# The down projection of a gated MLP, with products as the outer loop and output tiles inside

## The reference, cut to what matters

```python
def conv_ffn(h, w_up_l, conv_w_l, conv_b_l, w_down_l, buf):
    u = h @ w_up_l
    up = jnp.concatenate([buf.astype(u.dtype), u], axis=1)
    c = conv_b_l
    for j in range(CONV_W):
        c = c + up[:, j:j + L] * conv_w_l[j]
    a, b = jnp.split(c, 2, axis=-1)
    y = (jax.nn.silu(a) * b) @ w_down_l
    return y, up[:, -(CONV_W - 1):]
# per layer: x += RMSNorm_post(conv_ffn(RMSNorm_pre(x), ...)); everything in float32
```

## Time and profile before

| | before |
|---|---|
| median of 3 runs | 3350.73 us |
| the profiled execution, device time | 3351.13 us |
| its span in the trace | 3349.3 us |
| TensorE matmul busy | 3053.3 us, 91% |
| VectorE busy | 2233.6 us, 67% |
| ScalarE busy | 1498.5 us, 45% |
| GpSimd busy | 1177.3 us, 35% |
| DMA | 309.67 MB, mean 92 GB/s |

### The profile page before, as it was taken

One profiled execution on the slowest core, in us unless ns is written; L12 is line 12 of the kernel. 1 busy time (PEld: TensorE's weight loads), 2 busy tenths in 40 slices (PEclk: granted clock), 3 DMA queues, 4 the chain that ended last, 5 costly groups with the idle time before them and its releaser, 6 DMA issues. The chain is left out here.

```text
span 3349.3 us, 57862 instructions
## 1 busy us (share of the span) xinstructions
PE 3053.3 (91%) x23292; PEld 2903.8 (87%) x23292; DVE 2233.6 (67%) x3027; ACT 1498.5 (45%) x2616; POOL 1177.3 (35%) x664
## 2 busy tenths in 40 slices
PE   8999999999699999768889999999986999997677
PEld 8999789987599999768789997899876999997676
DVE  7887755443687777665587877563446877776665
ACT  6442554343455555433345426553434555554322
POOL 1111330111555555544411113301135555545443
PEclk9999999999799999889999999999998999998888
DMA  5112342216222223222321122421162222231223
GB/s 183 46 52 61 95 170 77 69 51 226 98 77 77 78 86 100 73 84 83 109 85 46 54 77 84 165 83 57 51 233 91 87 85 77 77 127 45 82 77 123
DMA packets 123304, 309.67 MB, mean 92 GB/s; under 512 B 9888, under 2 KB 69536, under 8 KB 119456
## 3 DMA queue, kind: packets, MB, share of 16 engines
q1 hardware_dynamic: 122752, 305.91, 27.4%
q10 hardware_dynamic: 288, 0.06, 0.0%
HBM read 245.91 MB, written 54.75 MB: 90 GB/s over the span
## 5 line engine op out<-in xcount | busy, mean ns | idle before, releaser
L325 PE MATMUL ps<-hh,w_hi 128*128 128x258 f32 (+3 forms) x4320 | 1352.0, 313 | 199.7 <-issue 73.2
L326 PE MATMUL ps<-hl,w_hi 128*128 128x258 f32 (+3 forms) x4320 | 1322.0, 306 | 0.0
L327 PE MATMUL ps<-hh,w_lo 128*128 128x258 f32 (+3 forms) x4320 | 1320.8, 306 | 0.0
L325 PEld LDWEIGHTS ps<-hh,w_hi 128*128 128x128 f32 x4320 | 835.3, 193 | 227.0 <-issue 167.7
L326 PEld LDWEIGHTS ps<-hl,w_hi 128*128 128x128 f32 x4320 | 837.4, 194 | 3.1 <-issue 0.5
L327 PEld LDWEIGHTS ps<-hh,w_lo 128*128 128x128 f32 x4320 | 834.7, 193 | 0.0
L310 POOL TENSOR_TENSOR w_lo<-w_raw,w_hi 128x1024 fp32r<-128x1024 f32 x134 | 349.8, 2614 | 1365.0 <-ACT w_hi L302 1365.0
L2262 POOL TENSOR_TENSOR w_lo<-w_lo_f,w_hi 128x512 fp32r<-128x512 f32 (+1 forms) x272 | 380.1, 1410 | 403.6 <-DVE w_lo_f L2921 301.9
L2262 POOL TENSOR_TENSOR w_lo<-w_raw,w_hi 128x512 fp32r<-128x512 f32 (+1 forms) x204 | 319.4, 1567 | 339.3 <-ACT w_hi L2625 336.2
L2625 ACT ACTIVATE w_hi<-w_lo_f 128x512 fp32r<-128x512 f32 (+1 forms) x272 | 167.8, 617 | 431.0 <-DVE w_lo_f L2921 430.8
L325 PE MATMUL ps<-Y_r,w_hi 128*128 128x258 f32 x1056 | 301.1, 285 | 16.4 <-ACT xT L2648 14.1
(11 more groups left out here) (381 smaller groups left out, 5085.4 us busy)
## 6 DMA issues: line engine op xcount, KB each, us to landing
w_raw<-in_w_stream SPq DMA_DIRECT2D x284, 512.0 KB, 3.6
gates<-f_c SPq DMA_DIRECT2D x44, 516.0 KB, 2.8
hl_f<-gates SPq DMA_DIRECT2D x24, 516.0 KB, 5.6
out_y_cols<-xT SPq DMA_DIRECT2D x6, 1376.0 KB, 8.4
xT<-out_y_cols SPq DMA_DIRECT2D x2, 4128.0 KB, 13.6
Y<-out_y_cols SPq DMA_DIRECT2D x12, 688.0 KB, 6.5
mem_keys<-in_cache_mem_k SPq DMA_DIRECT2D x6, 1024.0 KB, 5.3
Y<-in_cache_mem_k SPq DMA_DIRECT2D x6, 1024.0 KB, 8.0
```

The lines of the kernel that those rows point to most:

```text
L325: nc.tensor.matmul(out, whi, mhi, start=start, stop=False, skip_group_check=reopened)
L326: nc.tensor.matmul(out, whi, mlo, start=False, stop=False, skip_group_check=reopened)
L327: return nc.tensor.matmul(out, wlo, mhi, start=False, stop=stop, skip_group_check=reopened)
```

## The change

1. In the down part the order becomes group, product, output pair. A slot is one product of one group (`D_ORDER`: P_T1, P_22, P_11, P_T2, P_T3, P_T4, P_21); inside it the four output pairs `f` run for A and B, each pair and half in a PSUM bank of its own (bank 2f+p). A column operand is used in one slot only; when its slot is over, its gates for the next group are loaded, and combined and split in the slots that follow, by lists (`TODO`, `HIGHS`). All low parts of the column side in the down part are VectorE's.
2. The weight sums of the down part are made by GpSimd in units 2 to 21 of the up part, from raw weights loaded to the free part of `xT`, and kept in DRAM (`sums`). The down part loads each of its blocks by itself (`load_down`), the sums from there.
3. P_T2 lands in a buffer of its own (`Q`) and is merged into three quarters of the output by VectorE in the last group (`merge`).
4. The last slot runs all A steps before the B steps; the squares are taken by quarters in the last two slots, and the sums over partitions of the A quarters are put between the B steps.
5. In the up part's last unit (n = 21) VectorE combines the first operand of the down part (`combine_gates(0, P_T1, ..)`) right behind the gate, and the conv pieces are one behind the other.

```diff
+        sums = nc.dram_tensor("sums", (F_PAIRS * N_GROUPS, 4, P, 4 * P), F32, kind="Internal").ap()
...
+                    def load_down(d):
+                        g, c, f = DOWN[d]
+                        u, w = F_PAIRS * g + f, P * depth_in(g)
+                        sp.wait_ge(f_wlo, N_UP + d - 3 if d >= 4 else N_UP - 1 + d // 2)
...
+                            sp.wait_ge(f_kept, 16 * (u + 1))
+                            src = sums[u, (P_T1, P_T2, P_22, P_T3).index(c)][:, 0:w]
+                        sp.dma_start(down_raw(d), src).then_inc(f_draw[d % 4], 16)
...
+                    def load_gates(g, q):
...
+                            if q == "spare":
+                                if g:
+                                    sp.wait_ge(f_t, down_t_no(g - 1, P_T2, p))
+                                else:
+                                    sp.wait_ge(f_conv, 2 * (FT - 1))
...
+                                sp.wait_ge(f_step, STEP_NO[g - 1, q, F_PAIRS - 1, p] if g else STEP_NO[FT - 1, q, p])
...
+                    for n in range(FT):
+                        if n < FT - 1:
                             load_raw(n + 1, 0)
                             load_raw(n + 1, 1)
+                        else:
+                            for d in range(4):
+                                load_down(d)
+                        if n:
                             store_gate(n - 1)
+                        if n == 1:
+                            load_staged(0)
+                        for k in halves_in(n):
+                            if k % 2:
+                                store_sums(k // 2)
+                                if k // 2 + 1 < F_PAIRS * N_GROUPS:
+                                    load_staged(k // 2 + 1)
+                    for i, q in enumerate((P_T1, "spare", P_11, P_T2, P_22, P_T3, P_21, P_T4)):
+                        load_gates(0, q)
+                        if i >= 3 and i < 7:
+                            load_down(i + 1)
+                    for at_slot in range(NP * N_GROUPS):
+                        g, at = divmod(at_slot - 1, NP)
+                        if at_slot and g < LAST_G:
+                            load_gates(g + 1, D_ORDER[at])
+                            if at == 1:
+                                load_gates(g + 1, "spare")
+                        for d in range(4 * at_slot + 8, min(4 * at_slot + 12, len(DOWN))):
+                            load_down(d)
...
+                def halves_in(n):
+                    return [k for k in range(2 * F_PAIRS * N_GROUPS) if n == 2 + k * (FT - 2) // (2 * F_PAIRS * N_GROUPS)]
...
+                    def sum_half(k):
+                        i, half = divmod(k, 2)
+                        pool.wait_ge(f_stage, 32 * (i + 1))
...
+                    for n in range(FT):
                         if n:
                             low_block(n, P_T4)
+                        for k in halves_in(n):
+                            sum_half(k)
+                        if n < FT - 1:
                             for c in range(NP - 1):
                                 low_block(n + 1, c)
+                    for d in range(len(DOWN)):
+                        low_down(d)
+                    add_squares()
...
+                    def down_step(d, p):
+                        g, c, f = DOWN[d]
+                        nk, at = depth_in(g), D_ORDER.index(c)
+                        pe.wait_ge(f_wlo, N_UP + d + 1)
+                        if f == 0:
+                            pe.wait_ge(f_lo, down_low_no(g, c, p))
+                        if at:
+                            wait_down_read(pe, g, D_ORDER[at - 1], f, p)
...
+                    for p in (A, B):
+                        for f in range(F_PAIRS):
+                            down_step(len(DOWN) - F_PAIRS + f, p)
+                            if (f, p) == (1, B):
+                                end.sum_post(pe, 1)
+                                end.sum_post(pe, 0)
...
+                        if last:
+                            high_down(0)
+                            high_down(1)
+                            high_gates(0, P_T1, A)
+                            high_gates(0, P_T1, B)
+                            high_down(2)
+                            high_down(3)
...
+                    for n in range(1, FT):
+                        last = n == FT - 1
+                        conv(n - 1, 0)
+                        conv(n - 1, 1)
+                        gate(n - 1)
+                        if last:
+                            combine_gates(0, P_T1, A)
+                            combine_gates(0, P_T1, B)
+                        else:
                             combine_block(n + 1, P_T1)
                         add_out(n, P_22, A)
                         add_out(n, P_22, B)
...
                         add_out(n, P_T3, A)
                         add_out(n, P_T3, B)
+                        if last:
+                            low_gates(0, P_T1, A)
+                            low_gates(0, P_T1, B)
...
+                    c_, l_ = combine_gates, low_gates
+                    TODO = {1: [(l_, 0, P_11), (c_, 0, P_T3), (c_, 0, P_T2)], 2: [(c_, 0, P_T4), (l_, 0, P_T2), (l_, 0, P_T3)],
...
+                    for g in range(2, N_GROUPS):
+                        TODO |= {NP * g - 5: [(c_, g, P_T1)], NP * g - 4: [(l_, g, P_T1), (l_, g, P_22)], NP * g - 3: [(l_, g, P_11)],
+                                 NP * g - 2: [(c_, g, P_T3), (c_, g, P_T2)], NP * g - 1: [(c_, g, P_T4), (l_, g, P_T2)],
+                                 NP * g: [(l_, g, P_T3), (l_, g, P_T4)], NP * g + 1: [(l_, g, P_21)]}
+                    for at_slot in range(NP * N_GROUPS):
+                        g, at = divmod(at_slot, NP)
+                        c, todo = D_ORDER[at], [(*w, p) for w in TODO.get(at_slot, []) for p in (A, B)]
+                        if (g, c) == (LAST_G, P_T3):
+                            merge(0, A)
+                            merge(0, B)
+                        for i, (_, _, f, p) in enumerate(down_steps(g, c)):
+                            if down_read_by(g, c) == "dve":
+                                add_down(g, c, f, p)
+                            for do, *what in todo[len(todo) * i // 8:len(todo) * (i + 1) // 8]:
+                                do(*what)
+                            if (g, c) == (LAST_G, P_T3) and i % 2:
+                                merge(*MERGES[2 + i // 2])
...
+                    def sum_post(self, pe, q):
...
+                            pe.wait_ge(f_total, 2 * p + 8)
+                            pe.wait_ge(f_sq, 4 * p + 10)
```

More of the change, by code:

```diff
@@ L65, with depth_in, up_steps @@
 FIRST_TOUCH = (P_11, P_T1, P_T2, P_T4)
-def depth_of(n):
-    return 4 if n < FT + 2 * F_PAIRS else 3
-def steps_of(n):
+D_ORDER = [P_T1, P_22, P_11, P_T2, P_T3, P_T4, P_21]
+REOPENED = (P_22, P_T2, P_T4)
+D_FIRST = (P_T1, P_22, P_11, P_T2, P_T4)
+DOWN = [(g, c, f) for g in range(N_GROUPS) for c in D_ORDER for f in range(F_PAIRS)]
+N_UP = NP * FT
+NQ = N_UP + len(DOWN)
+LAST_G = N_GROUPS - 1
+def depth_in(g):
+    return GROUPS[g][1] // 2
+def up_steps(n):
     if n:
@@ L1102, in scalar @@
                     if end:
[L1103 to L1106, removed]
+                        end.root_post(act, 3)
+                        end.root_post(act, 2)
                         split_hi(act, load0 + 3)
@@ L1975, in t_no @@
[L1975 to L1993 removed]
+                T_DOWN = [P_T1, P_T3, P_T2, P_T4]
@@ new lines, in add_out, with add_down @@
+                        wait_read(dve, n, {P_22: P_T2, P_T3: P_T1, P_21: P_11}[c], p)
+                        to = landing(n, c, p)
+                        nc.vector.tensor_tensor(to, to, ps[:, bank_of(n, c, p), 0:QT], ALU.add).then_inc(f_rd, 1)
+                    def add_down(g, c, f, p):
+                        dve.wait_ge(f_step, STEP_NO[g, c, f, p])
+                        if c in (P_T3, P_21):
+                            wait_down_read(dve, g, {P_T3: P_T1, P_21: P_11}[c], f, p)
+                        else:
+                            wait_down_read(dve, g - 1, {P_T1: P_T3, P_11: P_21}.get(c, c), f, p)
+                        if g == LAST_G and c in (P_T3, P_T4):
+                            dve.wait_ge(f_merged, MERGES.index((int(c == P_T4), p)) + 1)
+                        to = down_landing(c, f, p)
+                        nc.vector.tensor_tensor(to, to, ps[:, 2 * f + p, 0:QT], ALU.add).then_inc(f_rd, 1)
@@ L3042, in vector @@
                         add_out(n, P_21, A)
                         add_out(n, P_21, B)
-                        if n < LAST:
+                        if not last:
                             combine_block(n + 1, P_T3)
-                        if after:
-                            for c, p in ((P_T1, A), (P_T1, B), (P_11, A), (P_11, B), (P_22, A)):
-                                low(after, c, p)
-                        add_out(n, P_T4, A)
-                        add_out(n, P_T4, B)
```

(1 more changed line is left out.)

687 lines of the change are left out of this document (381 added, 306 removed).

## The result

The changed kernel takes **3216.82 us** (median of 4 runs, 3212.28 to 3221.11) against 3351.65 us of the kernel before in the same session (3349.15 to 3355.02, 4 runs): a ratio of 0.9599, 95% interval 0.9588 to 0.9611, or 135 us less. The forecast was 3206 us, range 3178 to 3255. The profiled execution took 3216.17 us, with a span of 3214.4. By its page it moves 396.39 MB, where the kernel before moved 309.67.

The account below looks back on a forecast made before the run. TensorE, busy 91% of the span, was taken as the bound, losing 172.0 us at the down parts' group starts: 3351.1 - 172.0 + 2 x 10.4 + 2 x 1 + 2 x 2.4 = 3206.7, or 3206 us on the median's scale, range 3178 to 3255.

Parts of the forecast that it names:

- The stalls: At the three group starts of each layer's down part: TensorE's lost 172.0 us in both layers all return.
- Inside the groups: Down part within the groups and at groups two and three: 1 us a layer lost, up to 10 possible.
- Rival 2: VectorE sets the down part's pace: some 15 to 35 us a layer more, 3235 to 3280 us; chance 0.23.
- The entry: First group's start: TensorE idles 8.4 us before P_T4 for late gates, plus 2 us of slow clock; 10.4 a layer.
- The chain of 1 to 3 us of slack: Behind the entry, gates and low parts of the next operands are ready before TensorE wants them, by 1 to 3 us only.
- The up part: GpSimd's added weight sums in the up units cost 0 us, given 9 us of cover; bound 0 to 13 us.
- signs of being wrong: Over 3 us lost a slot in group two or three, an up unit over 20.15 us, or no P_T4 wait.
- Rival 3: Up units stretch as GpSimd waits for staged weights and sum stores; 3406 us at 5 us a unit; chance 0.02.
- The end: End of each layer: A's sums over partitions wait for squares, scaling begins 2.4 us later; bounds -4 and +8.

Follow-up runs that it names:

- e9: The changed kernel with VectorE's and ScalarE's operand work for the second and third group bunched in slot 6 of the group before; 3246.76 us, ratio 0.9686.
- e6: The changed kernel with each summed down-part block from the ninth on passed through VectorE again, 40 more operations a layer; 3226.77 us, ratio 0.9624.
- e2: e1 with SyncE's loads of P_T1's two summands issued ahead of the stores of gate 20 and the last sums; 3213.80 us, ratio 0.9595.
- e8: e7 with the first group's gates of P_21 and P_T4 loaded behind the third slot's first weight blocks; 3195.47 us, ratio 0.9531.
- e5: The changed kernel with GpSimd's up-part sums cut to 8 columns, their transfers and waits kept; 3213.73 us, ratio 0.9583.
- e3: The changed kernel with TensorE's two sums over partitions for A put behind all B steps instead of between them; 3208.21 us, ratio 0.9576.
- e7: The changed kernel with e4's and e3's edits together; 3201.12 us, ratio 0.9546.
- e1: The changed kernel with VectorE's two subtractions for P_T1 put behind the reads of P_22 and P_T3 in the last up unit; 3213.18 us, ratio 0.9591.
- e4: e2 with ScalarE reading P_T4's banks before rounding the fifth and sixth down blocks, and P_22's input and first weight block loaded ahead of other gates; 3211.71 us.

## Why the prediction was right, and where it was off

The forecast was 3206, the time 3217. By its steps:

- *The stalls, -172.0.* Right. (That *all* of it lay at the three starts was a little too strong: the three stretches of the earlier trace rows hold 83 of the first layer's 87 us.) 1802 matmuls in 216 us behind the entry, in both layers; e9 shows that they come back in part when the work is bunched.
- *Inside the groups, 1 us a layer.* Nothing was lost there. Rival 2 (VectorE sets the pace) fell: VectorE had 58 of 216 us to spare, and e6 put 15 of them to use for 4 us of time a layer. The rule that spoke for it, the Trainium skill's SBUF — State Buffer, section SBUF: two separate sides (a VectorE instruction with two SBUF inputs and a GpSimd one that reads SBUF shut each other out), fits the up part, where convolution operations take 2.05 us in the mean beside the sums and 1.28 without. It didn't become the bound in the down part.
- *The entry, 10.4 a layer.* Right in place, cause and size: 8.39 and 9.65 us idle against 8.4, the gates landed at +22.3 and +23.6 against +22, and 2.4 and 1.9 us went to the clock (matmuls 0.215 us apart from 1353.26 to 1358.12). By order of issue the loads were due at +22, and at +28 if the loads behind shared the engines with them. The Trainium skill, DMA: Bandwidth & Descriptors, section Queues, rings and completion order, has descriptors of one ring taken in order, and the trace agrees. The chain of 1 to 3 us of slack behind the entry held in the changed kernel. It has no room for more: where the entry was shortened, in e2 to e8, traffic at up to 375 GB/s held the next operands.
- *The up part, 0 (bound 0 to 13).* The term that was mis-sized in both layers: 2.3 and 2.2 us, counted from the up part's first matmul (905.16 and 2506.03) to unit 21 (1327.42 and 2928.2) against the same stretches before. I wrote that VectorE's instructions lengthen "say the gate's and one sum's"; they were the four convolution operations of a unit, some 0.8 us each, and VectorE went from 77 to 99.5% busy. The place was named, the read of P_T3 ahead of P_T4's step; its cover gave way in the units with four additions. These units of 20.7 to 21.2 us are one of the prediction's own signs of being wrong (an up unit longer than 20.15 us), and this term was. Rival 3's price of it (GpSimd's wait for staged weights) played no part: e5 kept the waits and the transfers.
- *The end, +2.4 a layer.* The kind was right (TensorE held between B's steps), and the size in sum: from unit 21's start to the scaling 258.5 and 260.8 us, forecast 260.0 and 259.5. The step that failed is what I didn't price: the passage behind the first layer's scaling. From scaling to the mixer's first matmul it is 13.85 us, before 9.25. ScalarE waits 6.93 us there for a weight slab (before 2.64), and eight residual operations take 5.96 us (before 3.99) beside a GpSimd split. In e3 it is 11.24 us, against 14.41 in the repeated run of the changed kernel, and ScalarE's wait for the slab falls from 7.50 to 4.33: 3.2 us of it were loads that came late with the held steps.
- *The remaining stages.* The first layer's came 2.8 us earlier, the second's mixer and attention 3.3 us later. Nothing in the change touches them, and the traces of the experiments, whose kernels are alike there, scatter as much: the first layer's up part starts at 903.6 to 908.4 us (before: 907.96), and from the mixer's first matmul to the second layer's up part it is 902.7 to 909.1 us (before: 902.98, changed kernel: 906.24). So these two terms are chance, and so is it that they nearly cancel.

Together, against the 144.4 us forecast between the two profiled executions: 4.6 (passage) - 1.4 (first layer's end) + 4.5 (up parts) + 3.3 - 2.8 (other stages) + 1.3 (second layer from unit 21 on) = 9.5, and 134.9 us is the difference of the spans.

## What to carry to other kernels

When several operands change at one boundary, ask first when each falls due: an order of the steps that makes them due one after the other hides most of their work, even where it is done in a lump. The wait that is left stands at the first boundary, and an earlier load helps there only as far as the next in-order queue (here ScalarE's weight split ahead of its reads) and the transfers allow. Work given to an idle GpSimd isn't free for VectorE: read VectorE's share before and after, and look for the units that got the most of it.

## What the runs showed of the hardware that I had not expected

- VectorE at 198.95 of 200 us busy cost TensorE only 10 matmuls of 1669 (0.6%), all in two of the ten units. A share near 100% was a warning and, in most units, not yet a stall.
- Near the entry the transfers ran at 335 to 365 GB/s over 10 us at a time in e7 and e8, and at 373 in one such stretch of e7's second layer (375 in e8's), with the 16 DMA engines' share at 0.99 to 1.09.
- A VectorE operation that was added cost less than its own time: 31.9 us of them in e6 (40 x 798 ns) raised VectorE's busy time by 15.
- After 8.40 us of idle time TensorE's granted clock was 0.50 for the next 5 us; after the 5.71 us of e1 it was 0.50 as well; in e8 it stayed at 1.00 from 1345 to 1357 through 2.52 us of idle time; in e7 the 10 us behind a wait of 1.93 us have a mean of 0.84. A wait of 2.48 us ahead of the sums over partitions left it at 1.00 in the repeated run of the changed kernel (1583 to 1585), and one of 2.47 us in the same place was followed by 0.50 in e4. So the length of a wait didn't decide by itself; what else did, no run shows.
